# A new order for the recurrent part and the second attention, and layer-ending products that wait tile by tile

## The reference, cut to what matters

```python
z = rms(x) @ w_in                    # split into the inputs of three branches and their gates
h = _mlstm(mq, mk, m_v, i, f)        # recurrent part: 4 heads, 4 chunks of 128 tokens
y_a = sigmoid(m_o) * _rms(h, m_norm_g)
y_c = _rms(_diff_attn(dq, dk, dv, lam), d_out_g) * (1.0 - lam_init)
y_b = _dsa(sq, sk, sv, iq, ik, i_w)  # second attention: 8 heads of 64, top-128 keys of an index score
merged = sum_i gates[i] * (y_i @ w_branch[i])
x = x + merged @ w_out
g, u = split(rms(x) @ w_gate_up)
x = x + (silu(g) * u) @ w_down
```

```python
dmat = where(causal, b[t] - b[s] + i[s], -inf);  inter = b + m_prev
m_t = maximum(inter, dmat.max(-1))
sw = exp(dmat - m_t) * (q @ k.T);  s_inter = exp(inter - m_t)
num = sw @ v + s_inter * (q @ c_prev);  den = sw.sum(-1) + s_inter * (q @ n_prev)
h = num / maximum(abs(den), exp(-m_t))
c_new = s_old * c_prev + s_loc * (k.T @ (w_loc * v))     # the state handed to chunk n + 1
```

## Time and profile before

| What | us |
|---|---|
| Median of three runs (lowest, highest) | 3265.07 (3262.32, 3268.91) |
| The profiled execution, its own time | 3263.64 |
| Its span, first to last instruction | 3261.8 |
| TensorE busy | 3039.7 (93%) |
| POOL busy | 1990.8 (61%) |
| VectorE busy | 1547.5 (47%) |
| ScalarE busy | 569.2 (17%) |

### The profile page before, as it was taken

The page is one execution under the profiler, slowest core; times in us unless marked ns, Lnnn a source line. Parts: engine busy times, 40 slices in busy tenths (PEclk is TensorE's granted clock), DMA queues, the critical chain, the costliest instruction groups (busy, mean ns, idle before and its releaser), DMA issues.

```text
span 3261.8 us, 38316 instructions
## 1 busy us (share of the span) xinstructions
PE 3039.7 (93%) x14046; PEld 2483.8 (76%) x14046; DVE 1547.5 (47%) x2547; ACT 569.2 (17%) x1178; POOL 1990.8 (61%) x2041
## 2 busy tenths in 40 slices
PE   8977988999999996898999999999999999999998
PEld 6866767888878875676778878777787888888876
DVE  6677773543333686786363333355430312223543
ACT  3223333110000322333210000000011211111000
POOL 6754433777767764344477777776676555555765
PEclk9998999999999998899999999999999999999999
DMA  4321211333323331111142333322233222322322
GB/s 136 97 69 43 59 49 55 119 91 96 101 81 100 120 91 56 45 59 49 59 129 91 98 97 89 98 86 80 85 97 103 78 78 78 97 78 71 97 84 77
DMA packets 87065, 274.64 MB, mean 84 GB/s; under 512 B 10384, under 2 KB 11025, under 8 KB 86929
## 3 DMA queue, kind: packets, MB, share of 16 engines
q1 hardware_dynamic: 85392, 270.71, 27.5%
q10 hardware_dynamic: 1536, 2.10, 0.3%
HBM read 266.48 MB, written 4.19 MB: 83 GB/s over the span
## 4 chain that ended last, share of the span: by engine, by line
PE 83%; DVE 12%; ACT 3%; issue 1%; DMA 0%; SPq 0%; DVEq 0%; POOL 0%; ACTq 0%
PE PS L435 55%; PE PS L484 13%; PE PS L722 3%; PE PS L730 3%; PE PS L783 2%; DVE MSK L1820 1%; ACT MS L1095 1%; DVE SMALLS L1819 1%; DVE MS L1865 1%; PE PS L984 1%; PE PS L448 1%; PE PS L771 1%; PE PS L760 0%; ACT TB L1095 0%; PE PS L959 0%
## 5 line engine op out<-in xcount | busy, mean ns | idle before, releaser
L397 POOL TENSOR_TENSOR POOL_C<-POOL_C 128x1 f32<-128x1 f32 x538 | 126.0, 234 | 1202.9 <-PE PS L435 640.5
L405 POOL TENSOR_TENSOR WL<-RAW,WH 128x512 fp32r<-128x512 f32 (+2 forms) x538 | 792.5, 1473 | 9.8
L435 PE MATMUL PS<-XNH,WH 128*128 128x512 f32 x1752 | 695.7, 397 | 14.0 <-DVE EYL L1514 9.5
L435 PE MATMUL PS<-XNL,WH 128*128 128x512 f32 x1752 | 686.0, 392 | 0.0
L402 POOL TENSOR_TENSOR WL<-RAW,WH 128x512 fp32r<-128x512 f32 x420 | 575.9, 1371 | 35.0
L398 POOL TENSOR_SCALAR WH<-RAW 128x1024 fp32r<-128x1024 f32 (+3 forms) x538 | 535.9, 996 | 0.2 <-issue 0.2
L435 PE MATMUL PS<-XNH,WL 128*128 128x512 f32 x1752 | 433.9, 390 | 0.0
L435 PEld LDWEIGHTS PS<-XNH,WH 128*128 128x128 f32 x1752 | 330.6, 189 | 88.8 <-DVE EYL L1514 10.7
L435 PEld LDWEIGHTS PS<-XNL,WH 128*128 128x128 f32 x1752 | 330.5, 189 | 71.4 <-issue 2.9
L435 PEld LDWEIGHTS PS<-XNH,WL 128*128 128x128 f32 x1752 | 327.6, 187 | 68.8
L484 PE MATMUL PS<-WH,XNH 128*128 128x512 f32 x704 | 277.5, 394 | 8.3 <-ACT TB L1095 3.8
(11 more groups left out here) (369 smaller groups left out, 4636.3 us busy)
## 6 DMA issues: line engine op xcount, KB each, us to landing
RAW<-w_oslot SPq DMA_DIRECT2D x56, 512.0 KB, 3.6
RAW<-w_L0ffn SPq DMA_DIRECT2D x44, 512.0 KB, 3.6
RAW<-w_L1ffn SPq DMA_DIRECT2D x44, 512.0 KB, 3.6
RAW<-w_od SPq DMA_DIRECT2D x32, 512.0 KB, 3.6
RAW<-w_epool SPq DMA_DIRECT2D x24, 512.0 KB, 3.6
RAW<-w_eug SPq DMA_DIRECT2D x16, 512.0 KB, 3.7
RAW<-w_eout SPq DMA_DIRECT2D x16, 512.0 KB, 3.6
RAW<-w_ovc SPq DMA_DIRECT2D x16, 512.0 KB, 3.6
```

The costliest lines, as they stand in the source:

```text
L397: nc.gpsimd.tensor_tensor(POOL_C[:, 1:2], POOL_C[:, 0:1], POOL_C[:, 0:1], ALU.add)
L405: nc.gpsimd.tensor_tensor(WL[:, half, at_:w], RAW[:, slot, at_:w], WH[:, half, at_:w].bitcast(F32), ALU.subtract).then_inc(S("weights_spli ...
L435: mm = nc.tensor.matmul(bank, w[:, slot, k * cols:(k + 1) * cols], x[:, k0 + k, :], start=first and j == 0 and w is WH and x is hi, stop=l ...
```

## The change

There are three parts.

**The recurrent part.** The diagonals, the weighted values, the division, the scaling in `norm_tile` of the second attention's keys, and the subtraction of the maximum go from VectorE to ScalarE. There each is a row of four operations of 128x128 or 128x129 (eight of 128x64 for the keys), scaled by a column. TensorE spreads the next chunk's diagonal right after n1, ahead of `half_of_keys(2n+1)`. VectorE does the maxima of chunk n+1 before it adds up n1 of chunk n and forms the state; n2 is taken after the key tile.

```diff
+                spread_u(0)
                 for n in range(NT):
...
-                    claim(b)
-                    pe.wait_ge(*L("diag_ready", n + 1))
-                    nc.tensor.matmul(PS[b][:, :], ONES[:, :], DG, start=True, stop=True
-                                     ).then_inc(L("ub_ready"), 1)
...
                     release[1] = release[0] = L("tot_ready", n + 1)
+                    if n < NT - 1:
+                        spread_u(n + 1)
                     half_of_keys(2 * n + 1)
```

VectorE's new loop (`maxima`, `total`, `state` and `denominators` hold the old instructions, without those that moved):

```diff
+                for n in range(NT):
+                    maxima(n)
+                    if n:
+                        total(n - 1)
+                        state(n - 1)
+                    dve.wait_ge(*L("pex_ready", n + 1))
+                    dve.wait_ge(*L("ms_ready", n + 1))
+                    V.tensor_tensor(DM, DM, PS[0][:, :], ALU.mult).then_inc(L("sw_ready"), 1)
+                    if n:
+                        denominators(n - 1)
+                    dve.wait_ge(*L("sk_scaled", 8 * n + 8))
+                    norm_tile(TA, n, None, sk_tables, "sk")
+                    if n:
+                        s_inter = args(n)[1]
+                        dve.wait_ge(*L("hall_ready", 4 * n))
+                        dve.wait_ge(*L("n2_ready", n))
```

The eight `WH` products now stand between the third turn and its values, and the four `WL` products between the fourth turn and its values. On ScalarE, in passes 1 to 7, the four exponentials of pass `q` no longer stand together ahead of the four `TB` copies of pass `q - 1`; they alternate:

```diff
                         if q < 8:
+                            exponential(0)
+                            if a == 0 or q == 0:
+                                for j in range(1, 4):
+                                    exponential(j)
...
                             for j in range(per):
+                                take_probs(j)
+                                if a == 1 and q < 8 and j < 3:
+                                    exponential(j + 1)
```

**The layer-ending products.** `down`, `eout` and `oout` no longer wait for the last input tile before they begin. In the first output column each `WH` product waits for its own input tile:

```diff
-                pe.wait_ge(*L("hidden_ready", KF))
-                residual(f"L{li}down", 2 * li + 1, (4, 5), [(6, 0), (6, 6), (5, 12), (5, 17)], HH, HL)
+                residual(f"L{li}down", 2 * li + 1, (4, 5), [(6, 0), (6, 6), (5, 12), (5, 17)], HH, HL,
+                         ready=lambda k: L("hidden_ready", k + 1))
...
-            pe.wait_ge(S("ey_ready"), 16)
-            residual("eout", 4, (3, 7), [(KD, 0), (KD, 8)], EYH, EYL)
+            residual("eout", 4, (3, 7), [(KD, 0), (KD, 8)], EYH, EYL, ready=lambda k: (S("ey_ready"), k + 1))
...
-            pe.wait_ge(S("od_ready"), 16)
-            residual("oout", 5, (0, 4), [(KD, 0), (KD, 8)], OYH, OYL)
+            residual("oout", 5, (0, 4), [(KD, 0), (KD, 8)], OYH, OYL, ready=lambda k: (S("od_ready"), k + 1))
```

More of the change, by code:

```diff
@@ L822, in layer @@
                         if q < 8:
-                            branch(name, i)
+                            branch(name, i, third_and_fourth if q and a == 1 else None)
+                        elif a == 1:
+                            third_and_fourth()
                         if q:
@@ L876, in pair @@
                                        last=q == per - 1, order=order,
-                                       ready=ready if isinstance(i, int) and t == 0 else None)
+                                       ready=(lambda j: ready(k0 + j)) if ready is not None and isinstance(i, int)
+                                       and t == 0 else None)
                 looped(pe, 4, pair)
@@ L1535, in ask_root @@
                     dve.wait_ge(*L("root_taken", ROOT_NO[name]))
-                    then(V.reciprocal((RSH if keep is None else keep)[:, 0:n], RSH[:, 0:n]))
+                    if keep is None:
+                        then(V.reciprocal(RSH[:, 0:n], RSH[:, 0:n]))
+                    else:
+                        V.reciprocal(keep[:, 0:n], RSH[:, 0:n]).then_inc(L("rsk_ready"), 1)
+                        dve.wait_ge(*L("rsk_ready", 1))
                 def squares(h, name, keep=None):
@@ L1698, in layer, with args, pair, maxima @@
                 squares(S_HEADS, "sk", keep=RSK)
-                for n in range(NT):
+                tot, ct = heads(TOT, 4), heads(CT, 4)
+                part_ = heads(YC[:, 0:2, :].rearrange("p a t -> p (a t)")[:, 0:516], 4)
+                def args(n):
+                    arg = ARG[:, 20 * n:20 * n + 20]
+                    return [arg[:, 4 * e:4 * e + 4] for e in range(5)]
+                def pair(b, e):
+                    return PS[b][:, 0:258].rearrange("p (h d) -> p h d", h=2)
+                def maxima(n):
                     h4 = slice(4 * n, 4 * n + 4)
-                    if n:
-                        diagonal(n)
                     ub = heads(PS[6 + n % 2][:, :], 4)
```

174 lines of the change are left out of this document (96 added, 78 removed).

## The result

The changed kernel takes 3190.5 us (median; 3188.4 to 3193.1), the kernel before 3263.7 on the same chip: a ratio of 0.9773 (0.9756 to 0.9790), 73 us less. The forecast was 3197.5, in a range of 3181 to 3221.

What follows compares the result with a forecast made beforehand. TensorE, busy 93% of the span, was taken to bound the kernel. Gains of 19.6, 21.2 and 26.5 sum to 67.3 us off 3263.6, leaving 3196.3; with 1.4 for the median, 3197.5 us, range 3181 to 3221.

Steps and rivals of the forecast that it cites:

- What bounds the kernel: Whole kernel: TensorE is busy 93% of the span, so only its idle or lower-clock places can give a gain.
- Part 1: Recurrent part: three turns shrink from 57.4 to 46.9 us, n1 starts 0.7 later; 19.6 us over both layers.
- the two delays of 1 us: Last recurrent turn: VectorE operations stretched while POOL works, 2 us added, making that turn 14.5 us.
- The wait of 8.88: TensorE's wait behind the recurrent part for VectorE's chain; it moves forward with n1, so does not eat the gain.
- The latency rule: Recurrent part's small ScalarE operations: at full 0.40 each instead of 0.30, the sum would be 5 us smaller.
- Part 2: Second attention: ScalarE's exponentials between copies and TensorE's new order shorten waits of `values`; 21.2 us.
- 6.0 + 5.2 - 0.6: Second attention, per layer: fewer exponentials before the first copy, later passes' waits gone, less re-entering `WL`; 10.6 us.
- Part 3: Layer-ending products `down`, `eout`, `oout`: waits for the last input tile and their clock cost go; 26.5 us.
- (a): Recurrent part gains nothing, new waits replacing the old ones; 3217 us, chance 0.22 including a part of it.
- (b): Recurrent part gains more: no delays, shorter waits keep the clock up throughout; 3188 us, chance 0.13.
- (c): Kernel slower: many short waits hold TensorE at 1.2 GHz through both recurrent parts; 3281 us, chance 0.03.
- (d): Layer-ending products: another wait, for weights or banks, stands behind the one removed; 3224 us, chance 0.05.

Runs made afterwards that it cites:

- late_spread: Changed kernel with TensorE spreading the next diagonal behind `half_of_keys(2n+1)` again, not ahead of it; 3218.3 us.
- only_part3: Kernel before with only the three `ready=` arguments, tile-by-tile waits of the layer-ending products; 3239.1 us.
- only_part1: Kernel before with only the change's edits of the recurrent part; 3246.6 us.
- turns_only_pe: Changed kernel with only TensorE's half of the second attention's new order; ScalarE does its four exponentials first, as before; 3215.5 us.
- better: Changed kernel with ScalarE's first diagonal earlier, chunk 2's `dk_raw` copies at its loop head, and VectorE's last key tile behind the last sum and denominators; 3178.6 us.
- better2: better with VectorE's first maxima ahead of the reciprocal of the roots and the first key tile scaled behind chunk 0's `SWT` copy; 3179.4 us.
- pool_held: better with one more POOL wait: the second half of one weight chunk's split is held until VectorE has finished the arguments; 3176.5 us.
- later_key_tile: better2 with each key tile turned one chunk later, the last two behind the last total; 3171.7 us.
- two_moves: better without the earlier first diagonal, so only the `dk_raw` copies and the last key tile are moved; 3178.0 us.

## Why the prediction was right, point by point

**What bounds the kernel** held. TensorE's busy share rose, and every gain was idle time or lower clock taken from it.

**Part 1** was forecast at 19.6 us and gave 17.3 alone. The turns gained 9.6 and 11.1 us where 10.5 were forecast. The terms of a turn add up to 13.65 and not 13.5; 13.42 was measured. Turn 1 came out as built from the rows, turn 3 too; turn 2 was 0.8 longer in the first layer and 0.3 shorter in the second. In turn 3 the two delays of 1 us did come, but in full-width operations of the key tile (1.52 and 1.64 in place of 0.69), not in those of four elements. The first spread waited 5.05 (forecast 4.7; the row at 199.48 is the second of a pair that began at 199.05, 0.4 sooner), `half_of_keys(4)` 3.32 (3.7), and n1(0) came at 215.24, of which 0.7 is a later start of the program, so 1.1 late (0.7). The wait of 8.88 in the earlier trace rows did not grow with the gain but fell to 7.86. The part does not work without the early spread, as late_spread shows, and I had not priced it apart. Nor did the forecast name the 16.7 us that the transposes of the weighted scores waited; it counted whole turns, and so held them all the same.

The latency rule that spoke against this part can be read now. ScalarE, first diagonal and first key tile:
```profile
203.54 1.26 ACT L1104 ACTIVATE MS<-IDENT,SMALLS 128x128 f32<-128x128 f32 x4
204.71 2.00 ACT L1104 ACTIVATE TA<-TA,SMALLS 128x64 f32<-128x64 f32 x8
```
Four of 128 columns take 1.26, so the next begins about 0.3 after the last (0.40 alone); eight of 64 take 2.00. The price of 0.30 held, partly by luck: the row that I took it from (438.10 to 438.40) is the step from an exponential to the reading of its own sum, not to a second operation of that size. The Trainium skill ("VectorE: DVE Perf Modes", section "The TRN2 errata — SBUF-src ops pay a fixed extra latency per instruction") says that many small tiles pay the latency per tile. Taken as the full 0.40 for each, as in the forecast's 5 us, the trace does not agree; in its direction it does, since four of 128 columns take 1.26 where one copy of 512 (from PSUM, at 214.51) takes 0.58.

**Part 2** was forecast at 21.2 and gave 27.8 alone, and 25 by the stage's starts in the traces (13.4 and 11.7). The mechanism was right; the mis-sized term is "6.0 + 5.2 - 0.6". The waits shown in the first layer fell from 16.1 to 5.5, 10.6 us, just the forecast of a layer; but each wait cost more than the trace shows as idle. The stretch of the part, before and then after:
```profile
441.00:567.00 126.00, 109.69 (x588) 85.94 (x588) 58.48 (x155) 36.53 (x99) 46.64 (x56) 0.98 0.17 52
```
```profile
433.00:546.00 113.00, 105.81 (x580) 84.62 (x580) 60.19 (x155) 37.40 (x103) 48.66 (x58) 0.98 0.19 56
```
TensorE is busy 3.9 us less for eight products fewer, at most 8 x 0.23 = 1.8. The other 2 us are "busy" time that carried no work: the last product ahead of a wait counts to its end, some 0.16 beyond the start of a successor that isn't there, and eleven of the layer's sixteen waits are gone. This share is worked out and no run separates it. The "0.1 per re-entered `WL`" (0.7 for seven passes, in the sum 0.6) did not show. The fourth head's copy, "just enough" covered, caused no wait in passes 1 to 7.

**Part 3** was forecast at 26.5 and gave 24.8 alone. By the starts of the stages `eout` gained 8.1 (8.0 forecast), `oout` 7.5 (7.8), the first `down` 5.6 (5.4) and the second 3.6 (5.4). The first output columns run at full clock. The second `down` itself gave its full share: from the last product ahead of it to its last `WH` product with `HH` it takes 119.9 us in the changed kernel and in only_part3, 125.4 before, 5.5 less, and the first `down` likewise. What is missing was lost in the even layer behind it, from there to the last product ahead of `eout`: 265.8 us in both kernels, 263.7 before. TensorE's waits in it are the same (18.2 us in all) and its busy time is 2.0 us longer: its stretches at the lower clock lie at other places now (the first 22 us behind `down` at a granted clock of 0.85, before at 1.00). So the four stages gave 26.8, and 2 went to the clock at a place that the change does not touch.

**The sum** came nearer than its parts. Parts 1 and 3 gave 2.3 and 1.7 less than forecast and part 2 6.6 more, 2.6 in all, and the whole change 5.9 more than the 67.3; that the time lies 7 us from the forecast owes something to these errors having two signs.

**The rivals.** (a) fell: part 1 gains. (b) named 3188, near the result, but its reason was wrong: VectorE's delays by POOL remained and the clock still dips; what came on top was part 2. (c) fell: the granted clock over the earlier trace rows's 75 us rose from 0.84 to 0.91, and it is 0.90 over 198 to 266 us, where the shorter recurrent part lies now. But late_spread shows its mechanism at work: behind a wait of 4.7 us in a turn (of 2.1 in only_part1) stands 1.2 GHz, behind those of 1.2 and 0.9 us 2.4 GHz. The length of the wait alone does not decide it. In the changed kernel n1 of the last chunk waits 3.38 us in the first layer, with 1.2 GHz behind it (2.09 for eight, shown above), and 3.40 in the second, with 2.4 GHz:
```profile
1264.17 1.16 PE L674 MATMUL PS<-VEXT,MS 128*128 128x129 f32 x8 [3.40 <-DVE MS L1842]
```
In turns_only_pe, too, a wait of 2.07 ahead of the scores (second layer) is followed by 1.16 for eight, where the 2.08 of only_part1 is followed by 1.94. (d) fell.

## What to carry to other kernels

Where a loop passes through several engines, find the step that closes it and move that: without the early spread the recurrent part gained nothing, and ScalarE's reordering took 10 to 11 us a layer off the second attention, while TensorE's own reordering alone took off 3 to 4 and nothing where the loop through VectorE was closed (the step from pass 2 to 3). Price a wait of TensorE above its shown idle time, by the drain ahead of it and, where it is long, by the lower clock that may stand behind it: in late_spread the turns lost two thirds of the displacement on top, most of it to the clock, but two waits of 3.4 us in the changed kernel had 1.2 GHz behind one and 2.4 behind the other. When an idle engine takes over small steps, look at what then falls together in time: the early first diagonal (better), the early maxima (better2) and the held split (pool_held) only moved the wait, and the first two paid once the key tile was out of the way (later_key_tile, 6 us under two_moves).

## What the runs showed of the hardware

**POOL holds VectorE's operations up, and a shift of under 0.1 us decides it.** The recurrent part up to here is the same code in only_part1 and in the whole change. VectorE's last operation of chunk 1's arguments in the changed kernel, and POOL:
```profile
220.29 0.16 DVE L1788 TENSOR_SCALAR SMALLS<-SMALLS 128x4 f32<-128x4 f32 x1
```
```profile
220.32 1.04 POOL L398 TENSOR_SCALAR WH<-RAW 128x1024 fp32r<-128x1024 f32 x1
```
In only_part1, where POOL is first:
```profile
220.04 1.02 DVE L1773 TENSOR_SCALAR SMALLS<-SMALLS 128x4 f32<-128x4 f32 x1
```
```profile
220.00 1.05 POOL L398 TENSOR_SCALAR WH<-RAW 128x1024 fp32r<-128x1024 f32 x1
```
Four elements take 0.16 or 1.02 us, up to the end of POOL's instruction, and n1(1) follows n1(0) after 13.4 or 16.0, since TensorE's wait of 2.1 then has the lower clock behind it. Between the two traces POOL's start moved from 0.03 behind that of VectorE's operation to 0.04 ahead of it. Full-width operations with two inputs from SBUF last up to 1.75 in place of 0.69 beside POOL's subtractions. Not every small operation beside POOL is held: in better2 one with two inputs from SBUF at 214.83 took 0.15 beside POOL's L398 (213.90 to 214.95), and the one at 215.09, beside L402, 1.23. The Trainium skill ("GPSIMD Engine Reference", section "8. Key points") says that GpSimd shares its SBUF interfaces with VectorE and contends with instructions in a 2-port perf mode or with two SBUF inputs. For the operations with two inputs the trace agrees (1.25, 1.11 and 1.75), but for that of 0.15, and adds the size. The operation that took 1.02 is a TENSOR_SCALAR with one input; whether it runs in such a mode no run here shows. The traces of only_part1 and two_moves lost 2.5 us in that turn by one such hold, so terms of 2 us in such a loop are at the edge of what a single profiled execution can size.
